# Two matmuls of 256 columns past the same weights made one of 512, in the up projection of a split-precision feed-forward layer

## The reference, cut to what matters

```python
D_FF = 2816
def swiglu_ffn(x, w_in, w_out):          # x: 256 x 1024, float32
    gate, up = jnp.split(x @ w_in, 2, axis=-1)
    return (jax.nn.silu(gate) * up) @ w_out
h = h + 0.5 * swiglu_ffn(rmsnorm(h, ffn1_norm[i]), ffn1_w_in[i], ffn1_w_out[i])
```

## Time and profile before

| | before |
|---|---|
| median of three timed runs | 1660.9 us |
| profiled execution | 1645.22 us |
| its span | 1643.4 us |
| mean granted TensorE clock | 0.899 |
| PE busy | 1486.4 us (90%) |
| weight loads (PEld) busy | 1359.8 us (83%) |
| DVE busy | 816.5 us (50%) |
| ACT busy | 688.8 us (42%) |
| POOL busy | 438.3 us (27%) |
| HBM read | 216.40 MB, 134 GB/s over the span |

### The profile page before, as it was taken

The page is one execution under the profiler, slowest core; times in us unless marked ns, Lnnn a source line. Parts: engine busy times, 40 slices in busy tenths (PEclk is TensorE's granted clock), DMA queues, the critical chain, the costliest instruction groups (busy, mean ns, idle before and its releaser), DMA issues.

```text
span 1643.4 us, 27720 instructions
## 1 busy us (share of the span) xinstructions
PE 1486.4 (90%) x10884; PEld 1359.8 (83%) x10884; DVE 816.5 (50%) x1253; ACT 688.8 (42%) x974; POOL 438.3 (27%) x262
## 2 busy tenths in 40 slices
PE   4999979979999889999779999699997997779967
PEld 2999979969999889999765556599997996778746
DVE  4644446754444364433464443444434478454674
ACT  3544443344444244444344333454443344334442
POOL 1433322133332443333113331133331003010220
PEclk9999999989999899999965557899998997989788
DMA  7677626746664356665210000566652451414102
GB/s 199 187 222 211 199 77 198 224 147 195 193 193 150 94 148 192 191 191 179 60 48 20 20 20 26 159 200 191 191 179 60 133 170 68 144 52 144 63 0 77
DMA packets 271627, 222.52 MB, mean 135 GB/s; under 512 B 8066, under 2 KB 252182, under 8 KB 271436
## 3 DMA queue, kind: packets, MB, share of 16 engines
q1 hardware_dynamic: 268176, 212.44, 42.8%
q0 software_dynamic: 2368, 7.60, 1.8%
q10 hardware_dynamic: 1020, 1.62, 0.3%
HBM read 216.40 MB, written 4.19 MB: 134 GB/s over the span
## 4 chain that ended last, share of the span: by engine, by line
PE 79%; DVE 10%; ACT 3%; DMA 2%; issue 2%; SPq 2%; POOL 1%; DVEq 0%; ACTq 0%; POOLq 0%
PE bank L591 21%; PE bank L592 20%; PE bank L593 20%; PE bank L576 3%; PE bank L719 3%; DVE arena L1333 2%; PE bank L755 2%; DVE rstd L1322 2%; DVE wal L1342 1%; DMA raw_a<-in_ffn_w_in 1%; POOL hnl L1815 1%; SPq L345 1%; PE bank L720 1%; PE bank L737 1%; PE bank L756 1%
## 5 line engine op out<-in xcount | busy, mean ns | idle before, releaser
L591 PE MATMUL bank<-hnh,wah 128*128 128x256 f32 (+1 forms) x2080 | 593.1, 285 | 58.9 <-POOL hnl L1815 50.0
L592 PE MATMUL bank<-hnl,wah 128*128 128x256 f32 (+1 forms) x2080 | 584.5, 281 | 0.0
L593 PE MATMUL bank<-hnh,wal 128*128 128x256 f32 (+1 forms) x2080 | 584.3, 281 | 0.0
L1822 POOL TENSOR_TENSOR wbl<-raw_b,wbh 128x1024 fp32r<-128x1024 f32 x102 | 289.1, 2835 | 729.4 <-ACT wbh L1003 729.4
L591 PEld LDWEIGHTS bank<-hnh,wah 128*128 128x128 f32 (+1 forms) x2080 | 399.6, 192 | 69.3 <-issue 48.8
L592 PEld LDWEIGHTS bank<-hnl,wah 128*128 128x128 f32 (+1 forms) x2080 | 398.7, 192 | 1.5 <-issue 1.4
L593 PEld LDWEIGHTS bank<-hnh,wal 128*128 128x128 f32 (+1 forms) x2080 | 398.2, 191 | 0.0
L1342 DVE TENSOR_TENSOR wal<-raw_a,wah 128x2048 fp32r<-128x2048 f32 (+1 forms) x129 | 291.9, 2263 | 182.9 <-ACT wah L996 181.0
L996 ACT ACTIVATE wah<-raw_a 128x2048 fp32r<-128x2048 f32 (+3 forms) x127 | 239.2, 1888 | 11.7 <-DMA raw_a<-in_ffn_w_in 9.1
L1397 DVE TENSOR_TENSOR gate_hid<-gate_hid,bank 128x256 f32<-128x256 f32 x88 | 37.1, 421 | 362.0 <-ACT gate_hid L1081 361.1
L591 PE MATMUL bank<-hidh,wbh 128*128 128x256 f32 x768 | 215.9, 281 | 0.9 <-DVE hidl L1367 0.9
(11 more groups left out here) (222 smaller groups left out, 1950.9 us busy)
## 6 DMA issues: line engine op xcount, KB each, us to landing
raw_a<-in_ffn_w_in SPq DMA_DIRECT2D x176, 512.0 KB, 5.1
raw_b<-in_ffn_w_out SPq DMA_DIRECT2D x88, 512.0 KB, 4.9
raw_a<-in_w_in_even SPq DMA_DIRECT2D x15, 1024.0 KB, 5.3
raw_a<-in_conv_w_in SPq DMA_DIRECT2D x24, 512.0 KB, 4.4
raw_a<-in_w_in_odd SPq DMA_DIRECT2D x11, 1024.0 KB, 5.3
raw_a<-in_w_kv SPq DMA_DIRECT2D x6, 1024.0 KB, 5.4
raw_b<-in_conv_w_out SPq DMA_DIRECT2D x8, 512.0 KB, 5.8
raw_a<-in_attn_w_q SPq DMA_DIRECT2D x4, 1024.0 KB, 5.6
```

The source lines that it names most:

```text
L591: mm(dst, wh, xh, start=start, stop=False)
L592: mm(dst, wh, xl, start=False, stop=False)
L593: return mm(dst, wl, xh, start=False, stop=stop)
L1822: g.tensor_tensor(wbl[:, s], raw_b[:, s], wbh[:, s].bitcast(F32), ALU.subtract).then_inc(S("b_lo"), 1)
```

## The change

Four edits.

1. `hnh` and `hnl` become two views of one tile `hn` [128, 8, 2, 256], so that for each k-tile the high and the low activations lie side by side, 512 columns. Two `split` calls of the attention stages that wrote them as flat 512-element rows now write three-axis tiles.
2. In `up`, the first two matmuls of a triple (high weights, high and low activations) become one matmul of 512 columns into a whole bank, the products with the high activations in columns 0 to 255 and with the low ones in 256 to 511. The third (low weights, high activations) adds to columns 0 to 255. Each half g has its own bank now, `bank[4 + parity + 2g]`, so banks 4 to 7 are used; `gu_ready` is raised once per half.
3. DVE adds the two column halves of each bank with a `tensor_reduce` into the new tile `gsum` (memory shared with `sqs`). ACT's silu reads the sum, and DVE's product takes silu and up value from SBUF. ACT still waits for both halves before `hi_a`.
4. PE's wait for `hcmp_ready` moves from behind the third FFN to ahead of it.

```diff
-        hnh, hnl = sb("hnh", [P, KT, T], F32R), sb("hnl", [P, KT, T], F32R)
+        hn = sb("hn", [P, KT, 2, T], F32R)
+        hnh, hnl = hn[:, :, 0, :], hn[:, :, 1, :]
         zero = sb("zero", [P, 512], BF16)
+        gsum = sqs[:, :].rearrange("p (g c) -> p g c", g=2)
...
-                    s, b = (n["sa"] + u) % 2, bank[4 + (n["ffn"] + u) % 2]
+                    s, b = (n["sa"] + u) % 2, 4 + (n["ffn"] + u) % 2
                     for g in range(2):
                         c = slice(g * P, (g + 1) * P)
                         for k in range(KT):
                             if i is FIRST and u == 0 and g == 0:
                                 wait_hn(k)
-                            m = mm3(b[:, g * T:(g + 1) * T], wah[:, s, k, c], wal[:, s, k, c],
-                                    hnh[:, k, :], hnl[:, k, :], k == 0, k == KT - 1)
-                    m.then_inc(S("gu_ready"), 1)
+                            mm(bank[b + 2 * g][:, :], wah[:, s, k, c], hn[:, k], start=k == 0, stop=False)
+                            m = mm(bank[b + 2 * g][:, 0:T], wal[:, s, k, c], hnh[:, k, :], start=False,
+                                   stop=k == KT - 1)
+                        m.then_inc(S("gu_ready"), 1)
...
             n["hn"] += 4
+            pe.wait_ge(S("hcmp_ready"), 2)
             ffn()
 
-            pe.wait_ge(S("hcmp_ready"), 2)
             norm()
...
                 def step(i, u, more_a=True, more_b=True):
-                    act.wait_ge(S("gu_ready"), n["ffn"] + u + 1 + 2 * i)
-                    act.activation(silu[:, (n["ffn"] + u) % 2, :], bank[4 + (n["ffn"] + u) % 2][:, 0:T], ACT.Silu
+                    act.wait_ge(S("gsum_ready"), n["ffn"] + u + 1 + 2 * i)
+                    act.activation(silu[:, (n["ffn"] + u) % 2, :], gsum[:, 0, :], ACT.Silu
                                    ).then_inc(S("silu_ready"), 1)
+                    act.wait_ge(S("gu_ready"), 2 * n["ffn"] + 2 * u + 2 + 4 * i)
...
                     hs, gs = (n["hid"] + u) % 2, (n["ffn"] + u) % 2
+                    for g in range(2):
+                        v.wait_ge(S("gu_ready"), 2 * n["ffn"] + 2 * u + g + 1 + 4 * i)
+                        x = v.tensor_reduce(gsum[:, g, :], bank[4 + 2 * g + gs][:, :].rearrange(
+                            "p (x c) -> p c x", x=2), AX, ALU.add)
+                        if g == 0:
+                            x.then_inc(S("gsum_ready"), 1)
+                        else:
+                            link(x)
                     v.wait_ge(S("silu_ready"), n["ffn"] + u + 1 + 2 * i)
-                    link(v.tensor_tensor(hf[:, hs, :], silu[:, gs, :], bank[4 + gs][:, T:2 * T], ALU.mult))
+                    link(v.tensor_tensor(hf[:, hs, :], silu[:, gs, :], gsum[:, 1, :], ALU.mult))
...
-                split(hnh[:, t2, :].rearrange("p t c -> p (t c)"), hnl[:, t2, :].rearrange("p t c -> p (t c)"),
-                      bqk[:, 2 * j:2 * j + 2, :].rearrange("p t c -> p (t c)"))
+                split(hnh[:, t2, :], hnl[:, t2, :], bqk[:, 2 * j:2 * j + 2, :])
```

More of the change, by code:

```diff
@@ L1405, in ffn @@
                     for u in range(2):
-                        link.n = i * 4 + (base + 2 * u)
+                        link.n = i * 6 + (base + 3 * u)
                         step(i, u)
-                link.n = base + 2 * (FC - 2)
+                link.n = base + 3 * (FC - 2)
                 for u in range(2):
@@ L1790, in c_norm @@
                     t2 = slice(2 * j, 2 * j + 2)
-                    split(hnh[:, t2, :].rearrange("p t c -> p (t c)"), hnl[:, t2, :].rearrange("p t c -> p (t c)"),
-                          c2)
+                    split(hnh[:, t2, :], hnl[:, t2, :], cq[:, 2 * j:2 * j + 2, :])
             attend("odd", c_norm).then_inc(S("mix_ready"), 1)
```

## The result

The changed kernel took 1668.27 us (median; 1664.76 to 1678.51), the kernel before 1659.72 beside it: ratio 1.0062, 95% interval 1.0036 to 1.0089. Timed again later on one chip with two experiments it was 1671.9 against 1652.84, ratio 1.0105 (1.0050 to 1.0161). Forecast was 1643, range 1630 to 1662. The profiled execution took 1665.01 us, span 1663.2 against 1643.4.

A forecast was written before the change was run, and what follows sets the result against it. The prediction took PE's matmul pace in the FFNs as the bound. 19.6 us saved in up projections less 1.3 for the moved wait gave -18.3: 1645.2 to 1626.9 profiled, plus 15.7 for timed runs, 1643; range 1630 to 1662.

The forecast's parts named there:

- I take 215 ns for a 512-column matmul: Up projection: start-to-start time of the merged matmul, bounds 213 and 227 ns; with a 256-column one, 328.3 ns a k-step for 340.0.
- the whole gain has to come out of those nanoseconds: FFN matmuls: columns unchanged, so only the 6.7 ns (11.1 in the third FFN) of each load-matmul pair not streaming can be saved.
- the down projection is untouched: FFN down projection: its pairs of weight load and matmul stay 113.3 ns apart, so it neither gains nor loses.
- keeps its pace: Up projection's 256-column matmul with low weights: stays at 113.3 ns, 117.8 in the third FFN.
- The upper bound I gave, 227: Up projection: unfavourable bound in ns for a 512-column matmul, equal to two matmuls of 256; total gain then 1 us.
- the -18.3 of the sum: Whole kernel: 19.6 us saved in the up projections less 1.3 us for the moved wait, on the profiled execution.
- Rival 1: FFN loops: the mixed 512 and 256 sequence is slow, down pairs at 117.8 ns; 17.7 us slower, 1679; chance 0.13.
- turning point of 335 ns a k-step: Up projection: k-step cost above which the change turns slower, with down pairs at 117.8 ns.
- The third FFN's gain: Third FFN's up projection: 332.8 ns a k-step for 353.3, 20.5 saved over 352 steps, 7.2 us.
- Rival 2: All FFNs: no change, because the pace drops to 117.8 ns a pair; 6.5 us gained, 1654; chance 0.13.
- the 2.3 of the prediction: Chain from up to down projection: about 2.3 us behind the last matmul, before about 1.95; no stall expected.
- 1.3 was taken: Ahead of the third FFN: cost in us of the moved `hcmp_ready` wait with `open_acc` queued behind it, bounds 1.0 to 1.8.

The follow-up runs named there:

- e4: Kernel before plus some 1100 extra matmuls in blocks of various widths behind its last transposes; 1770.98 us, which says nothing here; 512 columns alone took 234 ns each.
- e3: Changed kernel with each half's eight 512-column matmuls grouped ahead of its eight of 256, instead of alternating; 1661.45 us, ratio 1.0045 to the kernel before.
- e5: Kernel before, unchanged, profiled once more; 1652.90 us in one run, all four FFNs at 8.16 us a chunk.
- e2: Kernel before with only PE's wait for `hcmp_ready` moved ahead of the third FFN; 1650.34 us, ratio 0.9972 to the kernel before.

## Why the prediction was wrong

**The step that failed** is "I take 215 ns for a 512-column matmul", and under it "the whole gain has to come out of those nanoseconds", read as belonging to the pair. They go with the columns (e4). In the loop the 512-column matmul takes 235 ns, and at best (e3) 226, which is two of 256 at 113.3. A second step failed with it: "the down projection is untouched", and the low-weight matmul "keeps its pace". Both were put at their old pace without a loss and went from 113.3 to 117.8.

I took 213 from bf16 and 215 from a pass of a float32 matmul, both types other than the fp32r of the loop, and did not ask why the price per column should carry over. A row could have warned me: with 68 weight columns a pair still took 115.6 ns, so a smaller load did not bring the pair nearer to 106.7. The upper bound I gave, 227, was in truth the best case.

In the terms of the sum: 20.5 ns x 1408 = 28.9 us from the 512-column matmuls, 4.5 ns x 1056 = 4.8 from the 256-column ones beside them, 4.5 ns x 24 x 66 = 7.1 from the down projection, together 40.8. From the -18.3 of the sum to the 19.8 measured are 38.1; the first chunks of the first FFN, which do not run at this pace, make up 2.0 of the difference.

**Rival 1 was the truth, sized nearly right, and I gave it 0.13.** It said 350 ns a k-step and 117.8 for down; measured are 353 and 118. It said 17.7 us on the profiled execution; the spans differ by 19.8. (Its turning point of 335 ns a k-step comes out at 337 if redone with all four FFNs; nothing hangs on it.) I argued it away by the late bf16 weight load at L612, a true reading of a row, which explained that row's 0.35 us but not the 118 ns of the pairs behind it. Those pairs were the finding.

**The third FFN's gain**, 7.2 us of my 19.6, rested on its 117.8 being a property of that stage. It was chance (e5), and the change gained nothing there. Rival 2 saw that the pace might tip, but kept 215 ns for the 512-column matmul in it: 332.8 ns a k-step, where 353 came.

**What held.** The reduction takes 0.69 us (0.7 taken). From the start of the second one at 102.72 to the end of the split at 104.76 are 2.0 us, with the 0.3 ahead of it the 2.3 of the prediction, and PE never waits for it in the loop. The loads stay hidden at 208 GB/s. The gelu ahead of the third FFN now ends at 618.21, and the first up matmul starts at 619.60, 1.4 us behind it where it had started with it; 1.3 was taken. e2 shows the same wait alone: last silu of the second FFN to first of the third 90.2 us, 89.1 before.

```profile
617.88 0.33 ACT L1211 ACTIVATE hcmp<-bank 128x60 f32<-128x60 f32 x2
```

```profile
618.67 1.49 PE L600 MATMUL bank<-zero 128*128 128x512 bf16 x3 [7.18 <-ACT hcmp L1211]
619.60 0.99 PE L630 MATMUL bank<-hn,wah 128*128 128x512 f32 x1
```

PE was the bound, as predicted, and so nothing hid the error: the gain stood on one unit price, and that price came from rows of another type.

## What to carry to other kernels

A unit price holds for the operand type it was read from: before a sum is built on a shape that the trace lacks, look for the same type at any other width, and price per column before pricing per instruction. Merging matmuls that share weights saved nothing here, where the price went with the columns, and mixing lengths slowed the matmuls that were left alone. When identical code shows two paces in one trace, take further profiles before giving either of them a cause: here e5 alone would have shown that the place in the program does not decide.

## What was not expected of the hardware

- fp32r columns stream at 0.443 ns each at the 2.4 GHz level at best (256: 113.3 ns, with zero moving data too); at the 1.2 GHz level 256 columns take 0.21 us, which is one column a cycle.
- Back-to-back fp32r matmuls have two stable paces, 113.3 and 117.8 ns at 256 columns. A stage keeps its pace over 22 chunks, some 1500 matmuls. It is settled within six matmuls of PE's last wait or of the clock's rise (36 FFNs). Alternating 512 and 256 columns sets the slow one each time, and it followed 48 matmuls with zero weights once; what decides it otherwise, and what physically differs, is open.
- 384 columns in a row take 173 ns and 512 take 234, each over 0.443 ns a column; 256-column pairs with zero weights take 120.
- The granted clock of the attention stages between the third and the fourth FFN differs between executions of one kernel (0.67 and 0.64 on average, 280.5 and 290.4 us), and with it the time by more than a whole slow FFN costs.
